# A decoder layer on one core: attention values in column halves, four masks on GpSimd, sampled tokens in four column tiles

## The reference

```
h1 = LN1(alpha*x  + 0.5*SwiGLU_1(x))
h2 = LN2(alpha*h1 + W_out[attn_group(h1) | hgrn2_group(h1)])
y  = LN3(alpha*h2 + 0.5*SwiGLU_2(h2))

# attn_group, prompt: 8 query heads, 2 key/value heads of 64, blocks of 128 queries
score = sum_h w[t,h] * relu(q_idx[t,h] . k_idx[s]);  idx = top_k(score, 256) of the causal keys
s = q . k[idx] * 64**-0.5;  p = softmax(s);  o = p @ v[idx]

# hgrn2_group: 8 heads, state 64 x 64
S_t = diag(f_t) S_{t-1} + (1-f_t) i_t^T;  o_t = S_t^T q_t;  RMSNorm per head, times silu(gate)
```

## Time and profile before

| | us |
|---|---|
| median of 3 runs | 2456.79 (2456.51 to 2461.78) |
| the profiled execution's own time | 2454.58 |
| its span, first to last instruction | 2452.8 |
| TensorE busy | 2365.9 (96%) |
| VectorE busy | 1669.7 (68%) |
| ScalarE busy | 701.8 (29%) |
| GpSimd busy | 865.2 (35%) |

### The profile page before, as it was taken

How to read it: one execution, slowest core, us unless ns; L and a number is a source line. 1 busy time by engine, 2 the same in 40 slices (tenths; PEclk the granted TensorE clock), 3 DMA queues, 4 the chain that set the end, 5 groups by cost and what they waited for, 6 DMA issues and landing times.

```text
span 2452.8 us, 33405 instructions
## 1 busy us (share of the span) xinstructions
PE 2365.9 (96%) x12317; PEld 1940.7 (79%) x12317; DVE 1669.7 (68%) x2677; ACT 701.8 (29%) x1407; POOL 865.2 (35%) x924
## 2 busy tenths in 40 slices
PE   8999999999999999999998899999999999999996
PEld 7888888888887636777777777788878888888885
DVE  6675666578874178897787866336576665677886
ACT  2122222200023166772222255513222222210014
POOL 5354444446573021110000021414244444444570
PEclk9999999999999999999998899999999999999998
DMA  6021223274211113320000112121012221157301
GB/s 181 18 95 52 86 70 104 104 262 152 87 56 35 58 43 112 105 85 18 19 1 2 32 42 56 30 70 35 10 61 87 69 89 59 61 198 264 142 18 69
DMA packets 137151, 192.31 MB, mean 78 GB/s; under 512 B 18728, under 2 KB 85368, under 8 KB 136736
## 3 DMA queue, kind: packets, MB, share of 16 engines
q1 hardware_dynamic: 129328, 169.71, 20.7%
q0 software_dynamic: 7664, 20.47, 2.9%
HBM read 160.10 MB, written 30.06 MB: 78 GB/s over the span
## 4 chain that ended last, share of the span: by engine, by line
PE 86%; DVE 9%; issue 2%; ACT 1%; POOL 1%; DMA 1%; SPq 0%; DVEq 0%; POOLq 0%; ACTq 0%
PE ps L1982 38%; PE ps L2076 15%; PE ps L727 8%; PE ps L732 6%; PE ps L1089 4%; PE ps L977 2%; PE ps L2079 2%; PE ps L951 1%; PE ps L772 1%; PE ps L785 1%; PE ps L867 1%; PE ps L964 1%; PE ps L795 1%; ACT big L1156 1%; DVE big L1411 0%
## 5 line engine op out<-in xcount | busy, mean ns | idle before, releaser
L1982 PE MATMUL ps<-big 128*128 128x258 f32 x1760 | 412.2, 382 | 5.1 <-DVE big L2395 4.6
L1982 PEld LDWEIGHTS ps<-big 128*128 128x128 f32 x1760 | 334.2, 190 | 57.7 <-issue 7.8
L2247 ACT ACTIVATE down_weights<-ps 128x258 f32<-128x258 f32 x370 | 142.4, 386 | 702.1 <-PE ps L1982 702.0
L2515 DVE TENSOR_TENSOR down_weights<-ps,down_weights 128x258 f32<-128x258 f32 x330 | 139.5, 425 | 263.6 <-ACT down_weights L2247 188.5
L727 PE MATMUL ps<-acts,weight_ring 128*128 128x344 f32 x768 | 237.5, 459 | 0.0
L727 PEld LDWEIGHTS ps<-acts,weight_ring 128*128 128x128 f32 x768 | 141.8, 190 | 77.2 <-issue 12.2
L2076 PE MATMUL ps<-big,aux 128*128 128x258 f32 x840 | 192.2, 383 | 4.0 <-DVE big L2628 4.0
L2823 POOL TENSOR_TENSOR big<-weight_ring 128x256 f32<-128x256 f32 x100 | 75.9, 761 | 334.8 <-PE ps L1982 300.9
L2076 PEld LDWEIGHTS ps<-big,aux 128*128 128x128 f32 x840 | 159.9, 191 | 29.6 <-DVE big L2628 5.6
L732 PE MATMUL ps<-weight_ring,acts 128*128 128x256 f32 (+3 forms) x720 | 177.7, 402 | 0.0
L732 PEld LDWEIGHTS ps<-weight_ring,acts 128*128 128x128 f32 (+1 forms) x720 | 129.1, 184 | 33.8 <-issue 2.8
(11 more groups left out here) (447 smaller groups left out, 4518.0 us busy)
## 6 DMA issues: line engine op xcount, KB each, us to landing
big<-scratch_hidden SPq DMA_DIRECT2D x12, 2838.0 KB, 11.0
weight_ring<-ffn_wd SPq DMA_DIRECT2D x8, 2816.0 KB, 9.8
scratch_hidden<-down_weights SPq DMA_DIRECT2D x40, 516.0 KB, 2.8
weight_ring<-ffn_wg SPq DMA_DIRECT2D x20, 1024.0 KB, 7.8
weight_ring<-ffn_wu SPq DMA_DIRECT2D x20, 1024.0 KB
down_weights<-ffn_wd SPq DMA_DIRECT2D x4, 2816.0 KB, 20.2
weight_ring<-w_in SPq DMA_DIRECT2D x9, 1024.0 KB, 5.3
big<-x_prompt SPq DMA_DIRECT2D x8, 512.0 KB, 5.7
```

What stands on the lines that cost most here:

```text
L1982: last = M(PS[:, 3 * e + bank, 0:TQ], lhs[:, i, :], rhs[:, i, :], start=begin and i == 0, stop=end and i == n - 1, skip_group_check=True)
L2247: A(st(e, c), PS[:, 3 * e, 0:TQ], ACT.Copy).then_inc(cp_done, 1)
L2515: V.tensor_tensor(out, PS[:, 3 * e + bank, 0:TQ], st(e, part), ALU.add).then_inc(add_done, 1)
```

## The change

1. **Values in column halves.** A pair now consists of one head of each key/value head (w_in's query columns, `MIX` 4 and 5, are loaded in that order, and W_out's rows, with three DMAs for one). `pv_pair` has the 64 value columns of a key/value head as stationary operand and 128 columns of turned probabilities moving; the two heads of a pair go to the two column halves of the array, and the output comes out turned (features x queries), undivided. ScalarE copies it to OTA; VectorE spreads the reciprocals of the sums over 512 columns (`divisors`), TensorE transposes them (`turn_divisors`), and VectorE multiplies (`divide`). Up to step 31 there are three buffers for each kind of probabilities, and the order of steps on TensorE is another.
2. **Masks.** Those of blocks 4 and 5 are made by VectorE inside HGRN passes t = 1 and 2 (block 4's before in t = 2, block 5's in attention). Those of 6, 7, 3 and 2 are made inside attention by GpSimd (seven instructions each), with the count by ScalarE (`count_above`, in steps 4, 12, 20, 25) and the scan by VectorE (`rank_equals`, one step later).
3. **Sampled tokens' units** in four column tiles: four matmuls with 64 (kvi: 82) moving columns each, into PSUM partitions 0, 32, 64, 96, for one with 256 (328); ScalarE copies by four or five instructions.

Only the core of the diff is shown; "..." marks what is left out.

```
-        MIX += [[(w_out, SLAB * s, SLAB)] for s in (2, 3, 0, 1)]
+        MIX += [[(rows, SLAB * s, SLAB) for rows in w_out] for s in (2, 3, 0, 1)]
...
-               [(w_in, QB0, 256)], [(w_in, QB0 + 256, 256)], [(w_in, RF0, P), (w_in, RQ0, P)],
+               [(w_in, QB0 + HD * x, HD) for x in (0, 4, 1, 5)], [(w_in, QB0 + HD * x, HD) for x in (2, 6, 3, 7)],
...
+        MASK_ORDER = (4, 5, 6, 7, 3, 2)
+        COUNT_AT, RANK_AT = (4, 12, 20, 25), (5, 13, 21, 26)
...
+                def keep_above(k):
+                    j, s, ma, mb, least = mask_parts(k)
+                    G.tensor_scalar(mb, s, least, None, ALU.is_gt).then_inc(passed, 1)
+                    G.tensor_scalar(ma, s, least, None, ALU.is_equal).then_inc(passed, 1)
+                def keep_first(k):
+                    j, s, ma, mb, least = mask_parts(k)
+                    pool.wait_ge(ranked, k + 1)
+                    link(G.tensor_scalar(NEEDP[:, j:j + 1], CGP[:, j:j + 1], -1.0, float(TOPK), ALU.mult, ALU.add))
+                    link(G.tensor_scalar(mb, mb, NEEDP[:, j:j + 1], None, ALU.is_le))
+                    link(G.tensor_tensor(ma, ma, mb, ALU.mult))
+                    link(G.tensor_scalar(mb, s, least, None, ALU.is_gt))
+                    link(G.tensor_tensor(ma, ma, mb, ALU.add))
+                    G.tensor_scalar(s, ma, 1.0, -MASKED, ALU.subtract, ALU.mult).then_inc(masked, 1)
...
                 for j in range(16):
                     if j:
                         pool.wait_ge(at_exp, 3 * j)
+                    if j in (2, 4, 7, 9):
+                        k = (2, 4, 7, 9).index(j)
+                        keep_first(k)
+                        if k < 3:
+                            keep_above(k + 1)
...
+                        part = a // 4
+                        for c in range(4):
+                            last = M(PS[32 * c:32 * c + NB, unit_bank(u), 0:part], ACTS[:, k, SEQ:TOK],
+                                     slab(m, a)[:, k, part * c:part * c + part], start=k == 0, stop=k == DT - 1)
...
                 for j in range(b + 1):
-                    c = P + HD * (h // 4)
-                    last = M(PS[:, 2 + bi % 2, HD * h:HD * h + HD], probs_turned(i)[:, P * j:P * j + P], KV[:, j, c:c + HD],
-                             start=j == 0, stop=j == b)
-                last.then_inc(at_pv, 1)
+                    for e in range(2):
+                        rows = slice(64 * e, 64 * e + 64)
+                        last = M(PS[rows, 2 + bi % 2, HD * h:HD * h + P], KV[:, j, P + HD * e:P + HD * e + HD],
+                                 probs_turned(2 * q + e)[:, P * j:P * j + P], start=j == 0, stop=j == b)
+                last.then_inc(at_pv, 2)
...
+                q = i // 2
+                if i == 0:
+                    qk_pair(1)
+                elif i <= SHORT and i % 2 == 0:
+                    pv_pair(q - 1)
+                if i % 2 == (1 if i < SHORT else 0) and q + 2 < 32:
+                    qk_pair(q + 2)
+                if i > SHORT + 1 and i % 2:
+                    pv_pair(q - 1)
...
-                    if t == 2 and lv in (2, 3):
-                        keep_top(ORDER[0], lv - 2)
+                    if t in (1, 2) and lv in (2, 3):
+                        keep_top(MASK_ORDER[t - 1], lv - 2)
...
+            def rank_equals(k):
+                n = P * (MASK_ORDER[k + 2] + 1)
+                dve.wait_ge(passed, 3 * NBITS + 2 * k + 2)
+                dve.wait_ge(summed, 3 * NBITS + k + 1)
+                V.tensor_tensor_scan(MASK_B[:, 0:n], MASK_A[:, 0:n], MASK_A[:, 0:n], 0.0, ALU.add, ALU.max).then_inc(ranked, 1)
...
+                r = RSUM.unsqueeze(2).to_broadcast([P, H, HD])
+                V.tensor_tensor(rspread(bi).rearrange("p (h d) -> p h d", d=HD), r, r, ALU.max).then_inc(at_on, 1)
...
+                V.tensor_tensor(rows, rows, PS[:, 2 + bi % 2, :].rearrange("p (k t) -> p k t", t=P), ALU.mult).then_inc(at_on, 1)
...
                     sample_load(0)
                     mix(16)
-                    mix(17)
                     for t in range(4):
                         sample_store(t)
                         if t == 2:
                             mix(14)
+                    mix(17)
                     mix(15)
```

More of the change, by code:

```diff
@@ L951, in qk_pair @@
                         last = M(PS[:, k0, 0:min(512, n - c)], QT[rows, h // 2, P * b:P * b + P],
-                                 K3[rows, h // 4, c:min(c + 512, n)], start=True, stop=True)
+                                 K3[rows, e, c:min(c + 512, n)], start=True, stop=True)
                         if c + 512 >= n:
@@ L1107, in act_mixer, with sample_unit @@
             A(LB[:, 2, :], LB[:, 2, :], ACT.Sigmoid).then_inc(lb_sig, 1)
+            def sample_unit(u):
+                _, name, _, a, _, j = UNITS[u]
+                part = a // 4
+                func = ACT.Silu if name == "rg" else ACT.Copy
+                row = {"kvi": KV[0:NB, BLK, :], "ri": RIS[:, 256 * j:256 * j + 256], "rg": RG[0:NB, BLK, 256 * j:256 * j + 256]}[name]
+                for c in range(4):
+                    src = PS[32 * c:32 * c + NB, unit_bank(u), 0:part]
+                    n = min(part, 256 - part * c)
+                    if n < part:
+                        A(KIW[0:NB, BLK, :], src[:, n:part], func)
+                    last = A(row[:, part * c:part * c + n], src[:, 0:n], func)
+                last.then_inc(unit_out, 1)
             def unit(u):
@@ L1111, in unit @@
                 act.wait_ge(unit_done, u + 1)
+                if kind == "t" and x == BLK:
+                    sample_unit(u)
+                    return
                 rows = P if kind == "f" or x < BLK else NB
@@ L1636, in biggest @@
                 dve.wait_ge(at_qk, i + 1)
-                if i >= 2:
+                if h == 0 and b >= FIRST_TOPK:
+                    dve.wait_ge(masked, MASKED_AT[b])
+                if i >= 3:
                     dve.wait_ge(at_tr, buffer_free(i))
@@ L1676, in dve_mixer @@
                     outputs(3)
[L1677 to L1680 removed]
+                if i >= H and i % H == 1:
+                    divisors(i // H - 1)
+                if i >= H and i % H == (4 if i < SHORT else 5):
+                    divide(i // H - 1)
+                if i in RANK_AT:
+                    rank_equals(RANK_AT.index(i))
                 if 1 <= i // H <= 4 and i % H == 6:
                     sample_state(i // H - 1)
[L1683 removed]
+            divisors(7)
+            divide(7)
             dve.wait_ge(at_tr, 64)
@@ L1775, in mix @@
                 at = 0
+                if m >= 14:
+                    for (rows, c0, width), part, k in zip(MIX[m], (slice(0, HD), slice(HD, P), slice(0, P)),
+                                                          (slice(0, 4), slice(0, 4), slice(4, DT))):
+                        sp.dma_start(slab(m, SLAB)[part, k, :], rows[:, :, c0:c0 + width]).then_inc(ring_in[m % 4], 16)
+                    return
                 for w, c0, width in MIX[m]:
@@ L1920, in _ @@
                     sp.wait_ge(o_out, 32)
-                    sp.dma_start(OD8, o_s).then_inc(oa_in, 16)
+                    for g in range(GRP):
+                        sp.dma_start(OD8.rearrange("b (s g d) -> b g s d", g=2, d=HD)[:, g],
+                                     o_s.rearrange("b (g s d) -> b g s d", g=2, d=HD)[:, g]).then_inc(oa_in, 16)
                     sp.wait_ge(or_in, 16)
-                    sp.wait_ge(oa_in, 16)
+                    sp.wait_ge(oa_in, 32)
                     for half in range(2):
```

140 lines of the change are left out of this document (72 added, 68 removed).

## The result

The changed kernel takes 2461.96 us (median of 19 runs, 2459.95 to 2466.09), the kernel before 2457.83 (19 runs beside them): a ratio of 1.0015, interval 1.0009 to 1.0021. 2434 was predicted, 2418 to 2450. So a change that was to take 29 us of work from the busiest engine made the kernel 4 us slower, 0.15%, a difference that is small but outside the interval.

The account below looks back on a forecast made before the run. TensorE, busy for 96% of the span, was taken as the bound. The terms -29 +2 -1 +3 +6.7 -4.1 gave -22.4 us, from 2454.58 to 2432.2, and 2434 as median; range 2418 to 2450.

Parts of the forecast that it names:

- Values, -29: Attention's values in column halves: 0.24 us a pair and key block, 0.20 saved 144 times, -29 us.
- What the other loops give back: +2: Attention: ScalarE's and VectorE's work fits under the shorter pairs, except 2 us given back in blocks 2, 1 and 0.
- VectorE without the masks: -1 ... the scans of four stay: Attention: five masks leave VectorE, four scans stay; TensorE's 8.2 us wait for maxima shrinks, -1 us (0 to -6).
- GpSimd, +3: Attention: masks take GpSimd 24 us, 8.8 for block 7; sampled states' VectorE instructions wait for it, +3 us (0 to 8).
- GpSimd is late: Rival, attention masks: at 4.1 ns a column ScalarE's counts and TensorE wait, +17 us, 2474 us; chance 0.05.
- The port: Attention: GpSimd and VectorE exclude each other for whole instructions, holding up the states' instructions; without it the +3 would be 0.
- Masks in HGRN, +6.7: HGRN passes 1 and 2: block 4's mask in pass 1 costs 6 us, block 5's larger one in pass 2 0.7.
- Sampled units, -4.1: Sampled tokens' units in column tiles: kvi -2.7, rg in pass 1 -1, two of ri -0.4; ends -1 and -8 us.
- That in pass 3: HGRN pass 3: the shorter sampled tokens' unit stands before a level for which VectorE is late, 0 us.
- Loads, 0: Loading w_in's queries in 256-byte runs is covered before the slab's first unit; W_out's slot 1 loads later; 0 us.
- The signs of being wrong: Wrong if L1022's pace exceeds 0.3 us, ScalarE waits for GpSimd, or pass 1 keeps its 75.5 us.
- another engine takes over: Rival, attention: blocks 3 to 0 gain nothing and idle TensorE gets more half clock, -9 us, 2448 us; chance 0.20.

Follow-up runs that it names:

- e12: Changed kernel with e1's later scans, e8's six GpSimd masks, e7's wait, e9's unit, and HGRN's last output moved behind step 3's maximum: 2426.52 us, ratio 0.9866.
- e3: Changed kernel with all six masks back where the kernel before has them, by VectorE; halves and sampled tokens' units stay: 2460.30 us, ratio 1.0012.
- e10: Kernel before without VectorE's five masks in attention (blocks 5, 6, 7, 3 and 2): 2445.96 us, ratio 0.9947.
- e4: Changed kernel with the masks of blocks 6, 7, 3 and 2 left out altogether: 2445.32 us, ratio 0.9949.
- e1: Changed kernel with VectorE's scans one to seven steps later, and ScalarE's last two counts and GpSimd's parts of three masks moved: 2448.76 us, ratio 0.9963.
- e6: Changed kernel with ScalarE's counts of blocks 6, 3 and 2 one step earlier, scans unmoved: 2454.51 us, ratio 0.9989.
- e7: e1 with GpSimd's scaling of W_out waiting until VectorE has spread the divisors of block 1: 2440.94 us, ratio 0.9929.
- e2: Changed kernel with the masks of blocks 6, 7, 3 and 2 made by VectorE alone, where the kernel before has them: 2464.46 us, ratio 1.0030.
- e5: Kernel before with only the sampled tokens' five units changed to four column tiles: 2457.48 us, ratio 1.0000.
- e9: e5 with the unit of pass 3 (gates, second half) as in the kernel before: 2454.95 us, ratio 0.9990.
- e8: e1 with the masks of blocks 4 and 5 also made by GpSimd, ScalarE and VectorE's scan, in HGRN pass 2: 2443.98 us, ratio 0.9943.

## Why the prediction was wrong, point by point

- **Values, -29: right, and no gain.** The pace was the predicted 0.24 us, 0.2 less a pair than before, 144 times. TensorE's busy time in attention is 131.1 us in e12, the kernel with the fewest waits, for 159.3: 28.2 less, but at a clock of 0.98 for 0.95, so a few us of this are the clock's and that it meets the 29 is in part luck. In the changed kernel it was given back twice: 17.4 us more idle time, and 11.7 us because the same work took 142.8 us at a clock of 0.89 (131.1 in e12). -28.2 + 11.7 + 17.4 = +0.9; this is an account of the traces, not a measurement of each cause.
- **"What the other loops give back: +2": the step that failed.** It added up VectorE's busy time by block (17.64 us in the 24.3 left of block 7) and called that a fit. The sum fits, the order doesn't: VectorE's work comes in pieces of 2.8 us (a state), 3.3 (the output) and up to 4.6 (a mask's part), and TensorE waits for the maximum behind such a piece as soon as a pair's own work is shorter. Even the sum took the free time of the old loop, "7 us and more in blocks 4 to 7"; in the blocks as it had shortened them VectorE has 3.7 us left in block 4 and 3.0 in block 5, before any mask leaves. e3 shows the failure with every mask unmoved: 5.6 us longer, where this step had 27 shorter. Without masks, e10 and e4, the loop gains 6.7. With its five masks the wait costs 21 us in the new loop (e3, e4) and 9 in the old one (e10). No run has the new order of steps without the halves, so that their shares stay open.
- **"VectorE without the masks: -1 ... the scans of four stay": failed too.** I counted the scans' length, not their wait. 13.4 us of VectorE's time went into it, 9.9 behind ScalarE's count. e1 put a price on it, 13 us.
- **GpSimd, +3: mis-sized.** The 8.8 us for block 7 were 19.8, and the 24 us of all four masks 58, since a one-input comparison isn't a memset. The rival "GpSimd is late" had the right direction and 2.3 ns a column as its point; it was 2.8. But it named ScalarE's count as what stands waiting for GpSimd, which no trace shows (VectorE's scan stood), and the time of 2474 us was too dear: e6 shows that GpSimd's lateness alone made 5.4 us of wait, the place of the count the rest. Its chance of 0.05 was far too low: for a kind of instruction that no row showed, the ends were 0.93 and 4.1 ns a column, and I took the low one.
- **The port.** In the changed kernel the states' instructions stayed at 0.69 us: no GpSimd mask ran beside them. That they would be held, the ground of the 3 us, is shown only in little elsewhere: in e12 one of a state's four takes 1.41 us beside a comparison of 1024 columns. The place I didn't see was the new `divisors` with two inputs in SBUF beside the scaling of W_out, which was there before: 5.6 us, and 4.5 of attention (e7). The Trainium skill (SBUF — State Buffer, SBUF: two separate sides) has the port pair held for a full instruction. The trace agrees in that VectorE's instruction is held up by far more than a share: begun at 1557.75, it ends at 1563.3, just after the third of GpSimd's four scaling instructions of 2.0 us (from 1557.09; the third ends at 1563.1). Why it loses to three in a row no run shows.
- **Masks in HGRN, +6.7:** right within its range. Pass 1 is 4.6 longer with the mask than without (e2, e3). Pass 2, with block 5's mask for block 4's, is 0.8 longer in the changed kernel and 2.4 in e2, so 5.4 to 7.0 in all.
- **Sampled units, -4.1:** 0 (e5), and about -3 with the last one undone (e9), against a kernel before that scatters by as much. "That in pass 3", taken as 0, cost 3.4: TensorE has to wait for VectorE there anyway, and I took more idle time as free. It cost the clock of the next 18 us.
- **Loads, 0:** right as far as is seen: the scores began 3.3 us earlier, sooner than with the units alone (2.0, e5).
- **The signs of being wrong** missed it. The pace was 0.24, no ScalarE wait for GpSimd stands in the trace, and pass 1 took 79.3 us: by its three signs the prediction was right. None of them looked at TensorE's wait for maxima. The rival "another engine takes over" was the nearest in kind, idle time and half clock on TensorE; but it put the loss in blocks 3 to 0, and blocks 4 to 7 are where 20 us failed to come.

What stays open is how much of e7's 7.8 us is its own. Of the 10.9 us of waits that e12 has left, its trace puts 4.8 behind the four states, 3.1 behind three divisions and 1.4 behind a scan. A TensorE order that has more work between two maxima wasn't tried.

## What to carry to other kernels

Before taking work from the engine that sets the time, lay the longest uninterrupted piece of every other engine beside what is left of a period; sums over a block hide it. An instruction handed to other engines comes back as a wait at the place where its result is joined, so put the join steps later than the hand-over, and look at what stands ahead of the helper's part in its own queue. And idle time on TensorE isn't free: shortening filler work ahead of a wait cost more here than it saved, by the clock.

## What the hardware showed that I had not expected

- GpSimd's comparisons of 1024 columns took 2.85 us with one input and 2.36 us for a product of two; two operations in one instruction (L713) 3.64. One input was the slower one.
- One VectorE instruction of 512 columns took 5.59 us beside GpSimd's two-input instructions (7.45 in e8), 0.69 without. Beside masks in pass 2 the means of two groups of VectorE's instructions stretched by 13 and 32% only.
- A TensorE idle time of 2.2 us, with VectorE-bound work around it, was followed by 18 us at a granted clock of 0.51; with 2.5 us more of filler ahead of it that stretch was at 0.85 and 4.4 us shorter.
